# Prompt delta rule: the doubling levels on half of the columns

## The chip, the cores and the metric

The kernel runs on one core of a Trainium2 chip. The metric is device time in microseconds (us); the kernel before takes 3104.95 us, the median of 3 runs (3104.65 to 3108.51). PE is TensorE, DVE VectorE, ACT ScalarE, POOL GpSimd, SP the engine that only issues transfers.

## The reference, cut to what matters

One decoder layer is computed for 1024 prompt tokens and 64 sample tokens. The part that matters here is the gated delta rule of the prompt, for 4 heads of 128 by 128:

```python
kb = kc * bc[..., None]
m = jnp.where(strict, jnp.einsum('nbhid,nbhjd->nbhij', kb, kc) * decay, 0.0)
rhs = jnp.concatenate([vc * bc[..., None], kb * jnp.exp(gc)[..., None]], -1)
sol = lax.linalg.triangular_solve(m + jnp.eye(C), rhs, left_side=True, lower=True, unit_diagonal=True)
u, w = sol[..., :dv], sol[..., dv:]
# then, chunk after chunk: v_new = u - w S, o = (q e^g) S + qk v_new, S = S e^g_last + k' v_new
```

The kernel uses chunks of 128 tokens and does not solve the triangle row by row: it builds the inverse X of I + m by doubling the size of the blocks on the diagonal that are already inverted, from 1 to 128 in seven levels (0 to 6).

## The kernel before

The program is a row of stages with a barrier between each two. The change lies in one of them, `delta_prompt`. In it each engine has its own list of instructions in the order written, and waits on semaphores for the others.

Eight chunks are worked in four pairs `p`; the two chunks of a pair are the groups g = 0 and g = 1, with buffers of their own. Every tile is 128 partitions by 4 heads by 128 columns, so 512 columns for one instruction. For a pair the lists hold, in this order:

- Level 0: DVE multiplies `m` by the mask of level 0 into `ml` (`level_mask`, line 1725), and writes X = I - ml into `x` (L1732). PE turns X (L1496), ACT copies the result into `y` (L1611), so `y` is X transposed.
- Levels l = 1 to 6 (`level`, PE): t = ml[l]ᵀ y for g = 0 and then for g = 1 (L1547, 4 heads each, and each fp32 product is two passes, so 8 records); then for each group u = xᵀ tt (L1553) and the product for x, ttᵀ x (L1555), interleaved head by head. Between them ACT copies t from PSUM into `tt` (L1649). DVE's `update` subtracts u from `y` (L1772) and the other product from `x` (L1774); at level 6 only y is updated.
- DVE in level l: the masks of level l + 1 for both groups (L1725, 512 columns each), `update` for g = 0, `update` for g = 1, then other work that has been placed there: `gate_rows` of the next pair at l = 1 (L1686, two instructions), `decay_logs` of the next pair at l = 3 and l = 4 (L1695 to L1697, three instructions), and seven tiny instructions of a bit search for another stage (L2485 to L2487, L2390 to L2392, L2372). ACT does the counts of that search, two of 1028 columns for each level, after its two copies. PE has two wide matmuls for the next pair's gates after level 2 and two after level 3 (L1504).
- Between the pairs: the state is read, values and outputs of both chunks are made and the state is updated (L1514 to L1534 on PE, L1737 to L1761 on DVE), and the next pair's inputs are turned, scaled and multiplied (`scale_inputs`, `lower`, `first_x`). DVE's list ends this part with the mask of level 1 for g = 0, the outputs of the second chunk, and the mask of level 1 for g = 1.

PE's waits in `level` set the order around the change: t of group g at level l waits until `y` and `x` of that group are updated for level l - 1 and until its mask is made; u and the x product wait for ACT's copy.

The masks come from one line, and they say which columns can hold something:

```python
levels = [((i // (2 << l) == j // (2 << l)) & (i // (1 << l) % 2 == 1) & (j // (1 << l) % 2 == 0))
```

Row i must lie in an odd block of size 2^l and column j in an even one. So at level l half of the columns of `ml` are zero, in runs of 2^l.

Before the first pair DVE makes `gate_rows` of both chunks (L1686), copies the sums that PE made (L1780, L1782), and makes `decay_logs`, `scale_inputs`, `lower` and `first_x` of both. POOL only stores the outputs `o` of each chunk in this stage.

Of the kernel before, what the change touches and what calls it, by code (L numbers as in the profile page):

```python
# [1403 lines left out]
def over_heads(m):  # L1404

    return m.unsqueeze(1).to_broadcast([m.shape[0], GH, m.shape[1]])
# [6 lines left out]

def delta_prompt(nc, ident, ones, masks, qkv_in, beta, gate, unit, state, state_out, o_out, top, dump, squares):
# [7 lines left out]
    with ExitStack() as ctx:  # L1422
# [7 lines left out]
        ml = sc.sb("ml", [P, 2, LEVELS, GH, P])  # L1430
        sums, exps = sc.sb("sums", [P, 3, n_chunks, GH]), sc.sb("exps", [P, 3, n_chunks, GH])
# [16 lines left out]
        @block.gpsimd  # L1448
        def _(pool):
            def store(c):  # L1450
                pool.wait_ge(s["o_done"], c + 1)
                pool.dma_start(o_out[c], o[:, c % 2].rearrange("p h v -> p (h v)")).then_inc(s[f"o_stored{c % 2}"], 16)

            for c in range(n_chunks):
                store(c)
            for g in range(2):
                pool.wait_ge(s[f"o_stored{g}"], 16 * pairs)
# [144 lines left out]
        def _(act):  # L1602
# [38 lines left out]
            for p in range(pairs):  # L1641
                a, b = 2 * p, 2 * p + 1
                bit = p * bits
                for l in range(1, LEVELS):
                    for g in range(2):
                        act.wait_ge(s[f"t_done{g}"], 6 * p + l)
                        if l > 1 or p:
                            act.wait_ge(s[f"u_done{g}"], 6 * p + l - 1)
                        act.activation(tt[:, g], t_bank[g][:, :, :], ACT.Copy).then_inc(s[f"t_copied{g}"], 1)  # L1649
                    if p and l == 2:  # L1650
                        square_outputs(a - 1)
                    if p + 1 < pairs and l in (4, 5):
                        decays(2 * p + l - 2)
                    count(bit + l - 1, 0)
                    count(bit + l - 1, 1)
# [16 lines left out]
        def _(dve):  # L1672
# [46 lines left out]
            def level_mask(c, l):  # L1719
# [5 lines left out]
                dve.tensor_tensor(ml[:, g, l], m[:, g], over_heads(levels[l]), ALU.mult  # L1725
# [37 lines left out]
            def update(p, l, g):  # L1763
# [8 lines left out]
                dve.tensor_tensor(y[:, c % 4], y[:, c % 4], u_bank[g][:, :, :], ALU.subtract).then_inc(s[f"y_upd{g}"], 1)  # L1772
                if l < LEVELS - 1:
                    dve.tensor_tensor(x[:, g], x[:, g], x_bank[g][:, :, :], ALU.subtract).then_inc(s[f"x_upd{g}"], 1)  # L1774

            gate_rows(0)
            gate_rows(1)
            dve.wait_ge(s["totals"], 1)
# [1642 lines left out]
```

## Time and profile before

| | |
|---|---|
| median of 3 runs | 3104.95 us |
| the profiled execution: its own time / its span | 3107.7 us / 3105.9 us |
| busy share of PE, DVE, ACT, POOL | 91%, 50%, 29%, 7% |
| the stage `delta_prompt` in the span | 1485.4 to 1761.3 us: 275.9 us |
| PE, DVE, ACT, POOL busy in it | 226.1, 218.5, 138.5, 4.3 us |
| from the first level of the first pair to the last of the last | 1507.39 to 1737.71 us |

The profile page gives the busy time of each engine over the span and in 40 slices, and the costliest groups of instructions. The trace behind it answers for one stretch: the busy time of each engine between two times, the list of instructions in order of time with the idle time that an engine spent before each and the instruction that ended it, and the waits of one instruction for another, summed. An idle time that is not on the engine which everything else waits for costs nothing, so the stage is to be read level by level.

### The profile page before, as it was taken

What the parts mean: (1) busy time and instruction counts of PE and PEld (TensorE: products, weight loads), DVE (VectorE), ACT (ScalarE), POOL (GpSimd) and SP (SyncE); (2) the same over time, 40 slices, a digit from 0 to 9 for tenths busy, and PEclk for the clock granted to TensorE, in tenths of its full rate; (3) what the DMA queues carried; (4) which work ended last, traced back from release to release, by engine and by line L of the source; (5) the groups of instructions that cost most, each with busy time, mean ns of one, the idle gap of its engine ahead of it and who ended that gap; (6) DMA issues with size and microseconds to landing.
All of it is one profiled execution on the core that took longest, in us unless ns stands there. A gap on an engine that the chain in (4) does not pass through costs nothing. (4 is left out here: it accounts for less than half of the span.)

```text
span 3105.9 us, 44550 instructions
## 1 busy us (share of the span) xinstructions
PE 2813.8 (91%) x17345; PEld 2572.1 (83%) x17345; DVE 1552.0 (50%) x2393; ACT 889.7 (29%) x1450; POOL 221.8 (7%) x391
## 2 busy tenths in 40 slices
PE   7999999999959999868788788798879999999997
PEld 6999999999958799843687555468779999999997
DVE  5333333333444688738788678451354333333336
ACT  2111111111132557702455435341241111111111
POOL 0000000000000000015000000660000000000001
PEclk9999999999979999959899899898989999999998
DMA  3111111111031122234110101773011111111111
GB/s 108 55 41 41 45 44 48 48 42 36 6 111 35 49 74 70 85 87 103 50 43 11 53 14 32 214 224 112 14 41 55 41 54 41 43 45 46 41 41 58
DMA packets 264558, 186.55 MB, mean 60 GB/s; under 512 B 60303, under 2 KB 243807, under 8 KB 264390
## 3 DMA queue, kind: packets, MB, share of 16 engines
q1 hardware_dynamic: 212262, 112.33, 12.8%
q0 software_dynamic: 21440, 60.69, 6.0%
q10 hardware_dynamic: 30688, 11.27, 1.4%
q8 instruction: 108, 1.77, 0.2%
q14 instruction: 60, 0.49, 0.1%
HBM read 158.00 MB, written 26.22 MB: 59 GB/s over the span
## 5 line engine op out<-in xcount | busy, mean ns | idle before, releaser
L458 DVE TENSOR_TENSOR ffn_hidden<-ffn_hidden,ffn_ps_b 128x1092 f32<-128x1092 f32 x44 | 56.9, 1292 | 388.9 <-PE ffn_ps_b L85 388.9
L343 ACT ACTIVATE ffn_hi_d<-ffn_raw_d,ffn_row_mean 128x1024 fp32r<-128x1024 f32 x40 | 46.1, 1153 | 581.4 <-DVE ffn_row_mean L410 581.4
L359 ACT ACTIVATE ffn_h_hi<-ffn_hidden 128x1092 fp32r<-128x1092 f32 x44 | 49.3, 1119 | 485.3 <-DVE ffn_hidden L458 485.3
L85 PE MATMUL ffn_ps_a<-mixer_mix_hi,ffn_hi_g 128*128 128x364 f32 x528 | 117.7, 331 | 19.1 <-DVE ffn_lo_g L404 19.1
L205 POOL DMA_DIRECT2D ffn_raw_d<-in_ffn_w_down x40 | 21.3, 532 | 1593.2 <-DVE ffn_lo_d L419 1404.9
L85 PE MATMUL ffn_ps_a<-first_x_hi,ffn_hi_g 128*128 128x364 f32 x528 | 118.1, 332 | 9.5 <-DVE ffn_lo_g L404 6.1
L85 PE MATMUL proj_ps_a<-first_x_hi,proj_w_hi 128*128 128x364 f32 x336 | 79.1, 344 | 42.7 <-DVE proj_w_lo L1229 42.7
L85 PE MATMUL ffn_ps_a<-first_x_lo,ffn_hi_g 128*128 128x364 f32 x528 | 117.3, 331 | 0.0
L85 PE MATMUL ffn_ps_a<-mixer_mix_lo,ffn_hi_g 128*128 128x364 f32 x528 | 117.2, 330 | 0.0
L85 PE MATMUL ffn_ps_a<-first_x_hi,ffn_lo_g 128*128 128x364 f32 x528 | 117.0, 330 | 0.0
L85 PE MATMUL ffn_ps_b<-first_x_lo,ffn_hi_u 128*128 128x364 f32 x528 | 116.6, 329 | 0.0
L85 PE MATMUL ffn_ps_b<-first_x_hi,ffn_hi_u 128*128 128x364 f32 x528 | 116.5, 329 | 0.0
L85 PE MATMUL ffn_ps_a<-mixer_mix_hi,ffn_lo_g 128*128 128x364 f32 x528 | 116.5, 329 | 0.0
L85 PE MATMUL ffn_ps_b<-first_x_hi,ffn_lo_u 128*128 128x364 f32 x528 | 116.3, 328 | 0.0
L85 PE MATMUL ffn_ps_b<-mixer_mix_lo,ffn_hi_u 128*128 128x364 f32 x528 | 116.2, 328 | 0.0
L85 PE MATMUL ffn_ps_b<-mixer_mix_hi,ffn_hi_u 128*128 128x364 f32 x528 | 116.1, 327 | 0.0
L85 PE MATMUL ffn_ps_b<-mixer_mix_hi,ffn_lo_u 128*128 128x364 f32 x528 | 115.6, 327 | 0.0
L85 PE MATMUL ffn_ps_a<-ffn_h_hi,ffn_hi_d 128*128 128x364 f32 (+1 forms) x480 | 107.8, 333 | 5.5 <-DVE first_res L490 2.8
L85 PEld LDWEIGHTS ffn_ps_a<-mixer_mix_hi,ffn_hi_g 128*128 128x128 f32 x528 | 92.1, 190 | 20.2 <-issue 19.7
L2385 ACT ACTIVATE proj_spill<-main_scores_p,main_top_cand 128x768 bf16<-128x768 f32 (+2 forms) x96 | 99.0, 1034 | 33.5 <-DVE main_top_cand L2372 33.5
L352 ACT ACTIVATE ffn_hidden<-ffn_ps_a 128x1092 f32<-128x1092 f32 x44 | 47.6, 1083 | 212.1 <-PE ffn_ps_a L85 211.6
L85 PE MATMUL ffn_ps_b<-ffn_h_hi,ffn_hi_d 128*128 128x364 f32 (+1 forms) x480 | 106.2, 329 | 0.0
(645 smaller groups left out, 6975.4 us busy)
## 6 DMA issues: line engine op xcount, KB each, us to landing
ffn_raw_d<-in_ffn_w_down POOLq DMA_DIRECT2D x40, 512.0 KB, 3.7
proj_raw<-in_w_in SPq DMA_DIRECT2D x22, 512.0 KB, 3.8
second_ffn_raw_g<-in_ffn_w_gate SPq DMA_DIRECT2D x22, 512.0 KB, 4.1
second_ffn_raw_u<-in_ffn_w_up SPq DMA_DIRECT2D x22, 512.0 KB, 4.8
first_ffn_raw_g<-in_ffn_w_gate SPq DMA_DIRECT2D x21, 512.0 KB, 3.8
first_ffn_raw_u<-in_ffn_w_up SPq DMA_DIRECT2D x21, 512.0 KB
scratch_qkv<-proj_stage POOLq DMA_DIRECT2D x12, 544.0 KB, 3.0
delta_cur<-scratch_qkv SPq DMA_DIRECT2D x8, 768.0 KB, 5.3
```

Of the source, the lines that this page charges most:

```text
L85: last = pe.matmul(out[:, s, 0:USED[s]], w(k), x(k)[:, s * SL:s * SL + USED[s]], start=start and n == 0 and p == 0, stop=stop and n == len ...
L205: eng.dma_start(dst, src).then_inc(raw_in[kind], 16)
L343: act.activation(d_hi[:, k, :], raw["d"][:, :], ACT.Identity, bias=row_mean[:, k:k + 1]).then_inc(whi_done["d"], 1)
L352: act.activation(act_buf[:, fb, :].rearrange("p (s c) -> p s c", s=SLICES), ps_a[:, :, 0:SL], ACT.Silu).then_inc(silu_done, 1)
L359: act.activation(h_hi[:, par, fb, :], act_buf[:, fb, :], ACT.Copy).then_inc(hhi_done, 1)
L458: dve.tensor_tensor(hid, hid, ps_b[:, :, 0:SL], ALU.mult).then_inc(mul_done, 1)
L2385: act.activation(self.part(dump, i), self.score(i), ACT.Sign, bias=self.candidate(i), accum_out=self.count[:, i:i + 1]).then_inc(act_count ...
```

## The change

Masks, copies and updates of levels 1 to 6 are done on those 256 of the 512 columns that can be nonzero, through views that pick every second block of 2^l columns (`halves`). PE's matmuls keep their form and number.

- `level_mask` writes only the even blocks of `ml[l]` for l of 1 and above; level 0 is still done whole. The rest of `ml` must be zero: POOL clears all of it once, in two instructions of 3584 columns, before its first store, and DVE's first mask of each of the first two chunks waits for that.
- ACT copies only the odd blocks of t into `tt`. The rest of `tt` holds what earlier levels left there, so DVE clears `tt` once at the start, and ACT's first copy waits for that.
- `y` is updated in its odd blocks. `x` is updated in its even blocks, and since rows that are not in an odd block now get leftovers in the product, the update multiplies the product by -1 or 0 for each row: the subtraction becomes one SCALAR_TENSOR_TENSOR with a scalar for each partition, from the new tile `odd_rows`. DVE makes that tile at the start with five reductions over the masks and one small multiplication, which waits for the last of them, and the next instruction waits for the multiplication.

```diff
@@ -1411,6 +1411,16 @@
+def halves(v, l, odd):
+
+    return v.rearrange("p h (n a c) -> p (h n) a c", a=2, c=1 << l)[:, :, odd, :]
+
+
+def half_of_head(v, l, odd):
+
+    return v.rearrange("p (n a c) -> p n a c", a=2, c=1 << l)[:, :, odd, :]
@@ -1428,6 +1438,7 @@
         ml = sc.sb("ml", [P, 2, LEVELS, GH, P])
+        odd_rows = sc.sb("odd_rows", [P, LEVELS])
@@ -1451,6 +1462,8 @@
+            for g in range(2):
+                pool.memset(ml[:, g], 0.0).then_inc(s["masks_cleared"], 1)
             for c in range(n_chunks):
                 store(c)
@@ -1642,11 +1655,14 @@
                 for l in range(1, LEVELS):
+                    if l == 1 and p == 0:
+                        act.wait_ge(s["tt_cleared"], 1)
                     for g in range(2):
                         act.wait_ge(s[f"t_done{g}"], 6 * p + l)
                         if l > 1 or p:
                             act.wait_ge(s[f"u_done{g}"], 6 * p + l - 1)
-                        act.activation(tt[:, g], t_bank[g][:, :, :], ACT.Copy).then_inc(s[f"t_copied{g}"], 1)
+                        act.activation(halves(tt[:, g], l, 1), halves(t_bank[g], l, 1), ACT.Copy
+                                       ).then_inc(s[f"t_copied{g}"], 1)
@@ -1722,7 +1738,16 @@
-                dve.tensor_tensor(ml[:, g, l], m[:, g], over_heads(levels[l]), ALU.mult
+                if c < 2 and l == 0:
+                    dve.wait_ge(s["masks_cleared"], 2)
+                if l == 0:
+                    dve.tensor_tensor(ml[:, g, l], m[:, g], over_heads(levels[l]), ALU.mult
+                                      ).then_inc(s[f"level_made{g}"], 1)
+                    return
+                shape = [P, GH, P // 2 >> l, 1 << l]
+                mask = half_of_head(levels[l], l, 0).unsqueeze(1).to_broadcast(shape)
+                dve.tensor_tensor(halves(ml[:, g, l], l, 0).rearrange("p (h n) c -> p h n c", h=GH),
+                                  halves(m[:, g], l, 0).rearrange("p (h n) c -> p h n c", h=GH), mask, ALU.mult
                                   ).then_inc(s[f"level_made{g}"], 1)
@@ -1769,12 +1794,19 @@
-                dve.tensor_tensor(y[:, c % 4], y[:, c % 4], u_bank[g][:, :, :], ALU.subtract).then_inc(s[f"y_upd{g}"], 1)
+                yh, xh = halves(y[:, c % 4], l, 1), halves(x[:, g], l, 0)
+                dve.tensor_tensor(yh, yh, halves(u_bank[g], l, 1), ALU.subtract).then_inc(s[f"y_upd{g}"], 1)
                 if l < LEVELS - 1:
-                    dve.tensor_tensor(x[:, g], x[:, g], x_bank[g][:, :, :], ALU.subtract).then_inc(s[f"x_upd{g}"], 1)
+                    dve.scalar_tensor_tensor(xh, halves(x_bank[g], l, 0), odd_rows[:, l:l + 1], xh, ALU.mult, ALU.add
+                                             ).then_inc(s[f"x_upd{g}"], 1)
 
             gate_rows(0)
             gate_rows(1)
+            dve.memset(tt[:, :, :, :], 0.0).then_inc(s["tt_cleared"], 1)
+            for l in range(1, LEVELS - 1):
+                ins = dve.tensor_reduce(odd_rows[:, l:l + 1], levels[l], AX.X, ALU.max)
+            own(ins)
+            own(dve.tensor_scalar(odd_rows[:, 1:LEVELS - 1], odd_rows[:, 1:LEVELS - 1], -1.0, None, ALU.mult))
             dve.wait_ge(s["totals"], 1)
```

## Rows read from the trace of the kernel before

**Rows 1.** Busy time per stretch: levels 2, 3, 4, 5, 6 of pair 1.
```profile
1578.92:1586.05 7.13, 6.47 (x53) 5.83 (x52) 6.58 (x16) 4.63 (x14) 0.00 (x0) 1.00 0.00 1
1586.05:1592.32 6.27, 6.27 (x51) 5.80 (x50) 4.98 (x14) 3.46 (x6) 0.00 (x0) 1.00 0.01 1
1592.32:1598.98 6.66, 5.58 (x49) 5.41 (x48) 6.37 (x17) 4.63 (x7) 0.00 (x0) 1.00 0.01 2
1598.98:1605.97 6.99, 5.84 (x49) 5.51 (x49) 6.70 (x17) 4.63 (x7) 0.00 (x0) 1.00 0.00 0
1605.97:1609.97 4.00, 3.93 (x32) 3.77 (x33) 2.82 (x10) 2.24 (x5) 0.00 (x0) 1.00 0.00 0
```

**Rows 2.** Waits, 1507 to 1740 us: waiter, awaited, total us, times, longest us.
```profile
PE delta_bank_t L1547 <- DVE delta_x L1774: 11.8, 14, 1.1
PE delta_bank_t L1547 <- DVE delta_ml L1725: 5.5, 5, 1.4
```

**Rows 3.** Order of time, pair 3, end of level 3: start us, duration us, what.
```profile
1720.93 0.69 DVE L1772 TENSOR_TENSOR delta_y<-delta_y,delta_bank_u 128x512 f32<-128x512 f32 x1 [0.50 <-PE delta_bank_x L1555]
1721.54 0.68 DVE L1774 TENSOR_TENSOR delta_x<-delta_x,delta_bank_x 128x512 f32<-128x512 f32 x1
...
1722.36 1.13 PE L1547 MATMUL delta_bank_t<-delta_y,delta_ml 128*128 128x128 f32 x8 [0.66 <-DVE delta_x L1774]
```

**Rows 4.** The same view, pair 0, end of level 5.
```profile
1539.02 1.29 DVE L1725 TENSOR_TENSOR delta_ml<-delta_m,gdn_tab 128x512 f32<-128x512 f32 x2
...
1540.83 0.68 DVE L1774 TENSOR_TENSOR delta_x<-delta_x,delta_bank_x 128x512 f32<-128x512 f32 x1
...
1541.65 2.33 PE L1547 MATMUL delta_bank_t<-delta_y,delta_ml 128*128 128x128 f32 x16 [1.08 <-DVE delta_x L1774]
```

**Rows 5.** Groups of instructions, 512 columns: count, busy us, mean ns of one.
```profile
L1725 DVE TENSOR_TENSOR delta_ml<-delta_m,gdn_tab 128x512 f32<-128x512 f32 x56 | 36.6, 686 | 0.8
L1772 DVE TENSOR_TENSOR delta_y<-delta_y,delta_bank_u 128x512 f32<-128x512 f32 x48 | 32.9, 685 | 25.1 <-PE delta_bank_x L1555 20.2 <-PE delta_bank_u L1553 4.9
L1774 DVE TENSOR_TENSOR delta_x<-delta_x,delta_bank_x 128x512 f32<-128x512 f32 x40 | 27.2, 680 | 0.0
L1649 ACT ACTIVATE delta_tt<-delta_bank_t 128x512 f32<-128x512 f32 x48 | 28.6, 596 | 57.3 <-PE delta_bank_t L1547 57.3
```

**Rows 6.** The same view: 256 columns, from the sample tokens' delta rule.
```profile
L2028 DVE TENSOR_TENSOR sdelta_ml<-sdelta_m,sample_tab_s 64x256 f32<-64x256 f32 x3 | 1.1, 409 | 0.0
L2039 DVE TENSOR_TENSOR sdelta_y<-sdelta_y,sdelta_wide 64x256 f32<-64x256 f32 x2 | 0.8, 412 | 3.1 <-PE sdelta_b L1943 3.1
L1971 ACT ACTIVATE sdelta_kq_t<-sdelta_wide 128x256 f32<-128x256 f32 x1 | 0.4, 385 | 0.3 <-PE sdelta_wide L1905 0.3
```

**Rows 7.** The same view: with a scalar for each partition, two widths.
```profile
L1304 DVE SCALAR_TENSOR_TENSOR main_scores_p<-proj_spill,main_wi_tok,main_scores_p 128x512 f32<-128x512 f32 x21 | 15.1, 747 | 4.9 <-issue 2.8 <-ACT proj_spill L1130 1.9
...
L1304 DVE SCALAR_TENSOR_TENSOR main_scores_p<-proj_spill,main_wi_tok,main_scores_p 128x320 f32<-128x320 f32 x14 | 7.1, 547 | 4.1 <-ACT proj_spill L1130 2.7 <-issue 1.4
```

**Rows 8.** A copy in runs of 3 columns (min/median/max ns), and one without.
```profile
L1238 DVE COPY proj_xin<-proj_states x12: 171/176/181, 985.7 to 1181.6; 128x24 f32<-128x24 f32 x12
...
L1780 DVE COPY delta_sums<-delta_bank_t 128x64 f32<-128x64 f32 x1 | 0.2, 218 | 0.0
```

**Rows 9.** Order of time, start of the stage.
```profile
1488.45 0.69 DVE L1695 TENSOR_TENSOR delta_x<-delta_read,delta_sums 128x512 f32<-128x512 f32 x1 [1.28 <-PE delta_read L1504]
...
1499.83 0.69 DVE L1715 TENSOR_TENSOR delta_m<-delta_bank_t,delta_decay 128x512 f32<-128x512 f32 x1 [2.74 <-PE delta_bank_u L1488]
...
1501.77 0.68 DVE L1725 TENSOR_TENSOR delta_ml<-delta_m,gdn_tab 128x512 f32<-128x512 f32 x1
```

**Rows 10.** Groups of instructions elsewhere: a clear, a reduction, POOL's arithmetic.
```profile
L2246 DVE MEMSET ixs_qd<- 128x512 f32 x1 | 0.5, 485 | 4.5 <-PEq L3349 4.5
...
L2708 DVE TENSOR_REDUCE att_peak<-att_dots 128x1 f32<-128x128 f32 x8 | 2.3, 283 | 0.9 <-PE att_dots L2582 0.9
...
L800 POOL TENSOR_TENSOR ln_rows<-ln_rows,second_b_row 128x1024 f32<-128x1024 f32 x4 | 13.1, 3263 | 106.4 <-DVE ln_rows L819 106.4
```

## The prediction

> **What bounds the kernel now.** The page comes first: PE is busy for 91% of the span and DVE for 50%, so a change that leaves PE's matmuls alone can only win where PE stands and waits for somebody. The change lies in one stage of 275.9 us, so the next view is the busy time per stretch, cut at the first t product of each level [rows 1]. Read each row as length, then PE, then DVE. Three kinds of level are to be seen. Level 3 is 6.27 us with PE busy for all of it (it carries two extra gate matmuls): nothing to win. Level 2 has 0.66 us in which PE is not busy. Levels 4 and 5 have 1.08 and 1.15 us, and there DVE is busy for 6.37 of 6.66 and 6.70 of 6.99 us: DVE sets the pace, because `decay_logs` lies in its list. Who is waited for is in the summed waits [rows 2]: PE's t product waits 14 times for the update of x, 11.8 us in all, and five times for a mask, 5.5 us. The list in order of time shows the two forms of the first. In pair 3, after PE ends a level, DVE updates y and then x of group 1, and PE, having done t of group 0 meanwhile, stands 0.66 us until that is done [rows 3]. In pair 0, with decay logs in the list, the masks begin late, group 0's updates follow without a gap, and PE stands 1.08 us before t of group 0 [rows 4]. Eight waits of 0.66 and six of 1.08 make 5.3 + 6.5 = 11.8 us, which is the row's sum: four of the 0.66 precede level 2 (one for each pair), four lie in pair 3, which has no gate or decay work, and the 1.08 are the ends of levels 4 and 5 in pairs 0 to 2.
>
> **What half of the columns costs.** A mask goes from 686 ns to 409, the y update from 685 to 412 [rows 5, 6]; the rows of 256 columns are the same two operations in the sample tokens' stage, the second with PSUM as a source. The x update changes its form. With a scalar for each partition 512 columns take 747 ns and 320 take 547 [rows 7], 1.04 ns a column, so 256 take 547 - 64 x 1.04 = 480 ns against 680 now. ACT's copy goes from 596 to 385 ns. Savings: mask 0.28, y 0.27, x 0.20, copy 0.21 us. Those 256 columns come in runs of 2^l with as much left out between, down to 2 columns at level 1, and no row has runs of 2. The nearest has runs of 3: 24 columns in 176 ns, where 64 columns without gaps take 218 [rows 8]; 40 columns fewer at 1.04 give 176. So a run costs nothing that shows, and I take the prices above. The bound on the other side is that a short run costs as much as the columns it leaves out: then the half instruction takes as long as the whole one. Runs read from PSUM no row shows; they have the same two ends.
>
> **The sum, part by part.**
> (a) The eight waits of 0.66 us: the y and x updates of group 1 are the whole chain from the end of PE's products to t of group 1, so each shrinks by 0.27 + 0.20 = 0.47 and 0.19 stays. 8 x 0.47 = 3.8 us.
> (b) Levels 4 and 5 of pairs 0 to 2: DVE's list there loses two masks, two y and two x updates, 0.55 + 0.55 + 0.40 = 1.50 us, and its cycle falls from 6.98 to 5.48. PE without its wait needs 6.66 - 1.08 = 5.58, so PE is what is late next: level 4 takes 5.58, level 5 takes 5.58 and the remaining 0.19 of (a). That is 11.35 for 13.65, less 0.1 for a wait of that kind that level 6 may get: 2.2 for a pair, 6.6 us.
> (c) The first level of pairs 1 to 3: PE waits for the level-1 masks, five times. Each of these waits is one mask shorter, 5 x 0.28 = 1.4 us.
> (d) The part between the pairs: DVE settles a search bit before it goes on, and that waits for ACT's counts, which follow ACT's copies of level 6. Between 0 and 0.21 us for each of four pairs; I take 0.15, so 0.6 us. ACT's copies of the other levels are covered by t of the other group and bring nothing.
> (e) Added at the start, on DVE: a clear of 1024 columns, 2 x 0.485, five reductions of at most 0.283 [rows 10], and a tiny multiplication of at most 0.18 (the copy of 24 columns, rows 8), some 2.5 us. DVE stood idle 1.28 us just behind [rows 9], so `decay_logs` begins up to 1.3 us later. What of that reaches the first mask lies between 0 and 1.3, since DVE stands once more, 2.74 us, waiting for PE's products, which in turn wait for DVE's scaled inputs. I take 0.4. ACT's wait for the clear is over long before its first copy.
> (f) Added on POOL: two clears of 3584 columns. Their price no row shows. Its ends are 0 and POOL's arithmetic, 3.19 ns a column [rows 10], so 0 and 22.9 us for both; DVE's clear runs at 0.95 ns a column, 6.8 us for both, and being a clear it is the nearest. From the stage's opening at 1485.4 to the first mask at 1501.77 there are 16.4 us [rows 9], so I take no cost. Without that cover it is 22.9 - 16.4 = 6.5 us. Queued behind DVE's wait for it are all later masks, thus everything; behind the clears on POOL only the first store, at the end of pair 0.
> Together 3.8 + 6.6 + 1.4 + 0.6 - 0.4 = 12.0 us. The profiled execution took 3107.7 us with a span of 3105.9: it becomes 3095.7. The median lies 2.75 under that execution, so I give **3093.0**. No more can come than all waits of rows 2 and (d), 11.8 + 5.5 + 0.8 = 18.1 us, so not below 3087.
>
> **Rivals.**
> *POOL's clears are in DVE's way.* DVE's little multiplication comes at about 1489 us (where the idle time of rows 9 begins, 1487.2, with the 2.4 us of clear and reductions ahead of it, and the two small sums behind it instead of in front), while POOL is still clearing at the rate of (f). If it had to stand until the clears are over, at 1485.5 + 6.8 = 1492.3, everything behind would be up to 3.5 us later: 3096.5; with clears at POOL's arithmetic rate the first masks are 6.5 us late: 3099.5. For it: DVE's list at the start has hardly any slack. Against it: nothing in this stage shows the two engines at work at once, so the trace decides nothing. The Trainium skill has a rule for this case ("SBUF — State Buffer", section "Who interferes with whom"): a DVE instruction that uses two ports for one source, such as a multiplication by a constant from SBUF to SBUF, shares a pair of ports with GpSimd, and whoever issues first blocks the other for the whole instruction. By that rule the multiplication is such an instruction and the wait comes, while the clear of `tt` and the reductions pass. Chance 0.16.
> *Short runs are dear at levels 1 and 2 only.* Then five of the eight waits in (a) keep their length and so do the masks of (c): 2.4 + 1.4 less, 3096.8. Chance 0.09.
> *Slower: each run has a price.* The updates and masks on PE's path in (a) to (c) have some 2400 runs (1264, 360 and 768: for a y and x pair 256 at level 1, 128 at level 2 and so on down to 16 at level 5). From 12.0 / 2400 = 5 ns a run the gain is gone, from 7.6 the kernel is slower by over 0.2%; at 10 ns it would be 3105 - 12 + 24 = 3117. Against it: eight runs in rows 8 cost less than 1 ns each; for it, only that these runs are shorter and partly in PSUM. Chance 0.05.
> *The waits go but the time stays*, the change not doing what it says: PE would have to lose elsewhere what it gains, for instance by more of the first level at half of its clock, or ACT's counts would have to end last. In levels 2 to 6 of pair 1 the clock was whole, and ACT is busy 4.63 us at most in a level, under the 5.58 that PE needs. 3104 to 3106, chance 0.06.
>
> **How the numbers follow.** Forecast 3093, between 3088 and 3096.5 from (a) to (e), chance 0.64. The range 3087 to 3099 takes in the two first rivals and leaves out the last two. Two tenths of a percent, 6.2 us, is about what a measurement of this kernel can tell from no change, so faster means below 3098.7: the forecast, most of the first rival and the second, 0.64 + 0.12 + 0.08 = 0.84, rounded down to 0.82 for what I have not seen; within 0.2% 0.13; slower 0.05.
>
> **What would show it.** Masks and y updates of about 0.41 us and x updates of about 0.48, the same at level 1 as at level 5 (else the runs have a price); PE's waits for x near 0.2 us each and none of 1.08; levels 4 and 5 near 5.6 and 5.8 us; the first mask within 1 us of where it was, counted from the stage's opening, and DVE standing nowhere before its little multiplication; all other stages as before. It is wrong if DVE is seen standing beside POOL's clears, if level 1 alone stays long, or if PE's waits shrink and the stage doesn't.

## The result, and the profile after

The changed kernel takes 3087.24 us (median of seven runs, 3081.78 to 3091.53), the kernel before beside it 3103.30 us (seven runs, 3097.10 to 3108.51): ratio 0.9946, 95% interval 0.9935 to 0.9957. In a second comparison, with the experiments, it is 3089.55 against 3104.29 us, ratio 0.9959, interval 0.9945 to 0.9973. So it is faster by 13 to 16 us where 12.0 were forecast; 3087.24 us lies 5.8 us under the forecast of 3093.0 and below the 3088 that its terms allowed. The profiled execution of after took 3084.75 us with a span of 3083.1 us.

Single runs of one kernel lie some 4 us apart in stages that the change does not touch: in the first profile of after the stage opens at 1481.6 us, in the first of before at 1485.5, and in a second profile of before, taken later, at 1481.5. So stages are compared below, not spans. From the stage's opening to the read of the state in pair 3 it takes 252.2 and 253.1 us in the two profiles of before, 239.1 and 238.0 in the two of after: 14.1 us less in the mean.

The busy time per stretch of the first profile of after (stretch, length, then busy us of PE, PEld, DVE, ACT and POOL with the number of instructions, granted clock, share of the DMA engines, GB/s): the start, then levels 1 to 6 of pair 1, and the part between pairs 1 and 2, which I call the state part.

```profile
1481.50:1507.71 26.21, 17.48 (x88) 14.46 (x89) 21.36 (x39) 5.17 (x8) 6.10 (x2) 0.76 0.48 121
...
1568.30:1574.40 6.10, 5.73 (x49) 5.54 (x50) 4.17 (x14) 4.96 (x10) 0.54 (x1) 1.00 0.13 46
1574.40:1581.06 6.66, 6.45 (x52) 5.82 (x51) 5.27 (x17) 4.28 (x14) 0.00 (x0) 1.00 0.01 2
1581.06:1587.28 6.22, 6.22 (x52) 5.74 (x50) 3.52 (x14) 3.03 (x6) 0.00 (x0) 1.00 0.00 0
1587.28:1592.63 5.35, 5.35 (x49) 5.35 (x48) 4.74 (x15) 3.52 (x6) 0.00 (x0) 1.00 0.01 3
1592.63:1598.68 6.05, 5.76 (x50) 5.44 (x49) 5.31 (x16) 4.03 (x8) 0.00 (x0) 1.00 0.00 0
1598.68:1602.45 3.77, 3.77 (x32) 3.72 (x33) 2.36 (x10) 2.72 (x7) 0.00 (x0) 1.00 0.00 0
1602.45:1627.34 24.89, 19.00 (x162) 17.86 (x160) 20.74 (x45) 9.52 (x23) 0.54 (x1) 1.00 0.27 75
```

Against [rows 1], levels 2 to 6 of pair 1 are 7.13, 6.27, 6.66, 6.99 and 4.00 us before and 6.66, 6.22, 5.35, 6.05 and 3.77 after. In level 4 PE is now busy for the whole length (5.35 of 5.35) while DVE is busy for 4.74: the bound has gone from DVE back to PE, as step (b) said. The summed waits of PE show the same (waiter, awaited, total us, times, longest us), beside [rows 2]:

```profile
PE delta_bank_t L1560 <- DVE delta_ml L1749: 4.2, 5, 1.1
...
PE delta_bank_t L1560 <- DVE delta_x L1800: 2.3, 11, 0.2
```

The waits for x have gone from 11.8 us in 14 waits, the longest 1.1, to 2.3 us in 11, the longest 0.2. The five mask waits went from 5.5 to 4.2 us. The groups of instructions give the new prices, beside [rows 5] (count, busy us, mean ns of one):

```profile
L1798 DVE TENSOR_TENSOR delta_y<-delta_y,delta_bank_u 128x256 f32<-128x256 f32 x48 | 20.2, 420 | 38.8 <-PE delta_bank_x L1568 32.8 <-PE delta_bank_u L1566 5.8 <-issue 0.2
L1800 DVE SCALAR_TENSOR_TENSOR delta_x<-delta_bank_x,delta_odd_rows,delta_x 128x256 f32<-128x256 f32 x40 | 19.1, 478 | 0.0
L1664 ACT ACTIVATE delta_tt<-delta_bank_t 128x256 f32<-128x256 f32 x48 | 18.5, 386 | 49.2 <-PE delta_bank_t L1560 49.1
L1749 DVE TENSOR_TENSOR delta_ml<-delta_m,gdn_tab 128x256 f32<-128x256 f32 x48 | 18.4, 421 | 0.8
```

420, 478, 386 and 421 ns, where 412, 480, 385 and 409 were taken from other stages. All 48 masks lie between 416 and 426 ns, with runs of 2 columns as with runs of 64, and all y updates, which read PSUM, between 410 and 424: for DVE a run has no price that shows. ACT's copies take 383 to 385 ns at levels 2 to 6 and 378 to 414 at level 1, so there a run of 2 columns costs 0.03 us a copy at most.

Two rows of the first table are not in the forecast: the start is 26.21 us long where it was 21.99, and level 1 is 6.10 us at a granted clock of 1.00 where it was 7.94 at 0.79. The same view of the kernel before, its start and level 1 of its pairs 1 to 3:

```profile
1485.40:1507.39 21.99, 14.74 (x89) 11.29 (x89) 16.94 (x30) 5.17 (x8) 0.00 (x0) 0.81 0.56 144
1570.98:1578.92 7.94, 7.30 (x49) 7.11 (x49) 5.44 (x14) 4.98 (x10) 0.55 (x1) 0.79 0.09 35
1635.29:1643.29 8.00, 7.36 (x49) 7.17 (x49) 5.44 (x14) 4.98 (x10) 0.54 (x1) 0.79 0.09 34
1699.67:1708.09 8.42, 8.42 (x48) 8.40 (x49) 5.44 (x14) 5.09 (x10) 0.54 (x1) 0.64 0.09 33
```

The order of time at the start of after (start us, duration us, what, and in brackets the idle time before it and who ended it) shows why the start is longer:

```profile
1481.57 6.10 POOL L1466 MEMSET delta_ml<- 128x3584 f32 x2 [30.51 <-POOLq L3387]
1483.07 0.91 DVE L1805 MEMSET delta_tt<- 128x1024 f32 x1 [0.16 <-issue]
1483.89 0.99 DVE L1807 TENSOR_REDUCE delta_odd_rows<-gdn_tab 128x1 f32<-128x128 f32 x5
1484.92 2.78 DVE L1809 TENSOR_SCALAR delta_odd_rows<-delta_odd_rows 128x5 f32<-128x5 f32 x1
1488.10 0.68 DVE L1711 TENSOR_TENSOR delta_x<-delta_read,delta_sums 128x512 f32<-128x512 f32 x1
...
1500.16 0.69 DVE L1731 TENSOR_TENSOR delta_m<-delta_bank_t,delta_decay 128x512 f32<-128x512 f32 x1 [4.24 <-PE delta_bank_u L1501]
```

A multiplication of five columns takes 2.78 us and ends at 1487.70, in the moment in which POOL's clears do (1481.57 + 6.10 = 1487.67). Behind it the first decay log begins 6.5 us after the opening (3.0 before, [rows 9]). The clear and the five reductions run beside POOL in 0.91 and 0.99 us.

### The profile page after: what moved, and what is told of

Its sections match the earlier page's. It is cut to its first block and busy times, and to the rows that moved or that the text cites. A ratio compares the mean times of both kernels' runs of the same rounds, so it can differ in the third digit from the quotient of the medians.

```text
span 3083.1 us, 44548 instructions
## 1 busy us (share of the span) xinstructions
PE 2798.6 (91%) x17330; PEld 2561.9 (83%) x17345; DVE 1523.5 (49%) x2400; ACT 879.1 (29%) x1450; POOL 227.1 (7%) x393
## 5 line engine op out<-in xcount | busy, mean ns | idle before, releaser
L85 PEld LDWEIGHTS ffn_ps_a<-mixer_mix_hi,ffn_hi_g 128*128 128x128 f32 x528 | 92.1, 190 | 20.1 <-issue 19.6
```

The lines of the kernel that those rows point to most:

```text
L85: last = pe.matmul(out[:, s, 0:USED[s]], w(k), x(k)[:, s * SL:s * SL + USED[s]], start=start and n == 0 and p == 0, stop=stop and n == len ...
```

## The experiments

Theory A: the little multiplication has to stand until POOL's clears are over. Theory K: level 1 became shorter because PE waits less just ahead of it and so keeps its clock. The rivals are named in the expectations. e1 to e4, e6 and e10 are the changed kernel with one thing altered, e7 and e8 the changed kernel with several; e5 and e9 start from the kernel before, and two runs repeat after and before as they are.

### e1: the little multiplication in another form

```diff
-own(dve.tensor_scalar(odd_rows[:, 1:LEVELS - 1], odd_rows[:, 1:LEVELS - 1], -1.0, None, ALU.mult))
+own(dve.scalar_tensor_tensor(odd_rows[:, 1:LEVELS - 1], odd_rows[:, 1:LEVELS - 1], -2.0,
+                             odd_rows[:, 1:LEVELS - 1], ALU.mult, ALU.add))
```

> Edit: the little multiplication at the stage's start (L1809, five columns by -1, 2.78 us in the changed kernel) is written as a scalar_tensor_tensor of the same five columns (odd * -2 + odd), all else as in the changed kernel, POOL's clears with it. Theory A (a multiplication by a constant from SBUF to SBUF has to wait until POOL's clear is over, other forms don't): the new instruction takes 0.16 to 0.25 us and ends before 4 us from the stage's opening, while POOL clears until 6.1 us; the stage's start (opening to the first t product of level 1) falls from 26.2 us to between 23 and 24. Rival B (any DVE instruction at this place waits for POOL): still some 2.8 us and a start of 26.2. Rival C (the 2.78 us is the wait for the reductions' own semaphore or the price of the form, nothing of POOL): some 2.8 us, or a wait of that length ahead of it.

One run, 3088.79 us beside 3101.97 of before. The order of time:

```profile
1483.30 6.11 POOL L1466 MEMSET delta_ml<- 128x3584 f32 x2 [30.54 <-POOLq L3388]
...
1486.65 0.17 DVE L1809 SCALAR_TENSOR_TENSOR delta_odd_rows<-delta_odd_rows 128x5 f32<-128x5 f32 x1
```

0.17 us, ended 2.6 us ahead of the clears. The start is 22.5 us. Rival B falls, since another DVE instruction at this place does not wait, and of rival C the part that put the 2.78 us down to the reductions' semaphore. That the form is dear by itself, the rest of C, this run cannot exclude, because it changes the form; e2 and e6 can.

### e2: the set-up later

```diff
 gate_rows(0); gate_rows(1)
-<clear of tt, five reductions, little multiplication>
 ...
 search_start(0)
+<clear of tt, five reductions, little multiplication>
 for c in (0, 1):
     lower(c)
```

> Edit: clear of tt, five reductions and the little multiplication on DVE moved from the stage's opening to just ahead of lower(0), where DVE of the changed kernel stands 4.24 us for PE and POOL is long done. Theory A: multiplication 0.16 to 0.25 us; first decay log again 3.0 us behind the opening (6.5 in the changed kernel, 3.0 before), DVE's wait ahead of the first m shrinks to below 1 us, and the start falls from 26.2 to 22.0 (as before the change) or up to 0.4 above; the copy of the sums, an fp32 copy with PSUM as its source, runs beside POOL's clears in 0.22 us. Rival B (POOL's clears slow whatever DVE does): the copy or the decay logs take longer while POOL clears, start 24 to 26. Rival C (the multiplication is dear by itself): 2.8 us at the new place too, start near 22.5 to 24.

One run, 3091.21 us. The order of time:

```profile
1484.30 0.22 DVE L1807 COPY delta_sums<-delta_bank_t 128x64 f32<-128x64 f32 x1
...
1498.05 0.17 DVE L1821 TENSOR_SCALAR delta_odd_rows<-delta_odd_rows 128x5 f32<-128x5 f32 x1
1498.65 0.69 DVE L1731 TENSOR_TENSOR delta_m<-delta_bank_t,delta_decay 128x512 f32<-128x512 f32 x1 [0.43 <-PE delta_bank_u L1501]
```

The same instruction in its old form takes 0.17 us once POOL is done, so its form alone is not dear, and theory A is left. The copy out of PSUM runs beside the clears in 0.22, and all of the set-up fits into DVE's wait, of which 0.43 us are left. The start is 23.2 us, not the 22.0 to 22.4 that were expected: PE's transposes of the inputs took 1.06 us for four there. They take 0.60 in the first profile of before, whose start is 22.0, and 1.06 in most of the second, whose start is 22.8, so the start without the change scatters in the same way. In e7, with the same set-up, it is 22.0.

### e3: POOL's clears in fourteen pieces

```diff
 for g in range(2):
-    pool.memset(ml[:, g], 0.0).then_inc(s["masks_cleared"], 1)
+    for l in range(LEVELS):
+        pool.memset(ml[:, g, l], 0.0).then_inc(s["masks_cleared"], 1)
 ...
-dve.wait_ge(s["masks_cleared"], 2)
+dve.wait_ge(s["masks_cleared"], 2 * LEVELS)
```

> Edit: POOL's two clears of 3584 columns are cut into fourteen of 512, the same area. Theory A1 (the little multiplication waits for the one POOL instruction that is running): it takes at most 0.16 plus one short clear, 0.3 to 0.8 us, and the start falls by some 2 to 2.5 us to about 24. Theory A2 (POOL keeps the way as long as it has one clear behind the other): the multiplication ends when the last clear does, 2.8 us or a little more if fourteen clears take longer than two. If fourteen clears cost POOL much more than 6.1 us (over 0.15 us more for each), the first mask is still not reached before 20 us.

One run, 3085.40 us. The order of time:

```profile
1481.40 6.58 POOL L1467 MEMSET delta_ml<- 128x512 f32 x14 [30.53 <-POOLq L3388]
...
1484.75 3.25 DVE L1810 TENSOR_SCALAR delta_odd_rows<-delta_odd_rows 128x5 f32<-128x5 f32 x1
```

The multiplication stands through some seven of POOL's instructions, which follow each other every 0.47 us, and ends when the last one does (1488.00 and 1487.98). So A2 holds: cutting POOL's work into short instructions didn't let DVE in while one followed the other without a gap.

### e5 and e6: the two halves of the change alone

e5 keeps the half masks and POOL's clears, and takes back the copies, the updates and DVE's set-up; e6 keeps these and takes back the masks and the clears:

```diff
 e5:
-act.activation(halves(tt[:, g], l, 1), halves(t_bank[g], l, 1), ACT.Copy)
+act.activation(tt[:, g], t_bank[g][:, :, :], ACT.Copy)
-<half updates of y and x>
+<whole updates of y and x>
 e6:
-for g in range(2):
-    pool.memset(ml[:, g], 0.0).then_inc(s["masks_cleared"], 1)
-if l == 0:
+if l >= 0:          # every mask whole
```

> Edit: of the change only the half masks (and POOL's clears they need) remain; copies and updates are whole as before, without the clear of tt, the reductions and the little multiplication. By the prediction's own terms: DVE's list in levels 4 and 5 loses two masks, 0.55 us for each level, 3.3 us in pairs 0 to 2; the level-1 mask waits lose 1.4 us; the eight waits of 0.66 stay. Sum 4.7 us, so 0.9985 of the kernel before; stage start as before, 22.0 to 22.7 us, since nothing of the two-port form stands beside the clears. Theory K2 (the clock at level 1 of pairs 1 to 3 falls by chance, less often with the shorter mask waits: so far in 8 of 12 levels with half masks it stayed at 1.00, in 1 of 6 with whole ones): two of three level 1 at about 7.0 or below, some 2 us more, 0.998. Rival (masks gain nothing until the updates are short as well): levels 4 and 5 stay at 6.66 and 6.99, 0.9995 or more.

> Edit: of the change only the half copies and updates remain (with the clear of tt, the reductions and the little multiplication on DVE); masks are whole and POOL clears nothing. By the prediction's own terms: eight waits of 0.66 become 0.19 (3.8 us); DVE's list in levels 4 and 5 loses two y and two x updates, 0.94 us, so these levels are 5.7 and 6.05 long (1.9 us a pair, 5.7 us); state part 0.3; start 0.4 to 1.3 dearer. Sum 8.5 to 9.4 us, 0.997. Theory A for the start: without POOL's clears the little multiplication takes 0.17 us at its old place (2.78 in the changed kernel) and the start is 22.5 to 23.3 us instead of 26.2. Rival: it still takes 2.8. The clock at level 1 of pairs 1 to 3: with the long mask waits (1.42 and 0.65) it should mostly fall, 7.4 to 8 us a level, as before the change; if it stays at 1.00 in two of three, the length of the wait says nothing.

e5: 3097.01 us against 3104.29, ratio 0.9975, interval 0.9965 to 0.9985. e6: 3093.80 us, ratio 0.9960, interval 0.9945 to 0.9975. The busy time of levels 4 and 5 of pair 1 in e5:

```profile
1589.33:1595.47 6.14, 5.58 (x50) 5.42 (x48) 5.85 (x17) 4.36 (x6) 0.00 (x0) 1.00 0.01 3
1595.47:1601.92 6.45, 5.83 (x48) 5.51 (x49) 6.16 (x17) 4.64 (x8) 0.00 (x0) 1.00 0.00 0
```

The same two levels in e6:

```profile
1587.42:1593.14 5.72, 5.52 (x49) 5.36 (x48) 5.35 (x16) 3.88 (x6) 0.00 (x0) 1.00 0.01 3
1593.14:1599.36 6.22, 5.60 (x49) 5.44 (x49) 5.93 (x17) 4.21 (x8) 0.00 (x0) 1.00 0.00 0
```

Two masks fewer take 0.52 and 0.54 us from these levels (0.55 expected), two y and x updates fewer 0.94 and 0.77 (0.94). Each half pays by itself, as it should where DVE's list is the bound. Together with level 6 they save 1.05 and 2.06 us a pair, and both at once 2.48: the last 0.6 us are lost because PE is late by then. Level 1 of pairs 1 to 3 in e5 takes 6.84, 6.12 and 8.37 us, so theory K2's two of three came. The starts are 22.7 and 22.6 us. The little multiplication of e6, at its old place and with no clears on POOL:

```profile
1487.10 0.17 DVE L1805 TENSOR_SCALAR delta_odd_rows<-delta_odd_rows 128x5 f32<-128x5 f32 x1
```

In e6 POOL's clears and the half masks are gone, and with them the 2.8 us; in e5 the clears are there and no instruction of that form. Both agree with A, and e6 speaks once more against rival C.

### Level 1 and its clock: e4, the repeats, e9 and e10

e4 makes only the level-1 masks whole again:

```diff
-if l == 0:
+if l <= 1:
```

> Edit: only the level-1 masks are whole again (512 columns), four halves of the change stay. It puts the 0.28 us for each mask back into the wait ahead of the first t product of pairs 1 to 3. Theory K (the unforeseen gain at level 1 is the clock: PE stands 1.14 and 0.37 us in the changed kernel, 1.42 and 0.65 before, and with the shorter wait the granted clock of this level stays 1.00 where it was 0.79): level 1 of pairs 1 and 2 goes back from 6.10 us at 1.00 to 7.6 to 7.9 at about 0.8, so 1.3 to 1.8 us for each pair with two masks at 0.28 in it. Rival (the clock differs from run to run whatever the wait): level 1 at 6.1 to 6.7 us with a clock of 1.00, so at most 0.56 us a pair.

One run, 3086.82 us. Level 1 of pairs 1, 2 and 3:

```profile
1568.69:1576.12 7.43, 7.16 (x49) 6.86 (x50) 4.44 (x14) 4.61 (x10) 0.54 (x1) 0.77 0.10 37
1629.35:1635.72 6.37, 5.73 (x48) 5.54 (x49) 4.45 (x14) 4.57 (x10) 0.54 (x1) 1.00 0.11 42
1688.96:1696.01 7.05, 7.05 (x49) 7.03 (x50) 4.45 (x14) 4.68 (x10) 0.54 (x1) 0.77 0.11 40
```

One kernel, the same instructions, and the level is 6.37 us at 1.00 or 7.05 to 7.43 us at 0.77: PE's 5.73 us of work become 7.1 when a part of it runs at 1.2 instead of 2.4 GHz. Theory K in its strict form (a longer wait always lets the clock fall) does not hold for pair 2. So the next runs asked whether it is chance alone. A second profile of each kernel:

> The changed kernel as it is, beside the others: 0.9946 of the kernel before (0.9935 to 0.9957 earlier). In its profile: start 24 to 26.5 us with the little multiplication at 2.8 us again; level 1 of pairs 1 to 3 either near 6.1 us at a clock of 1.00 or near 7.1 to 7.4 at 0.77. Theory K2 (chance): not the same pairs as in the first profile (there pairs 1 and 2 at 1.00, pair 3 at 0.76). Rival (fixed by place): again pair 3 alone.

> The kernel before as it is, for a second profile. In question is level 1 of pairs 1 to 3, whose clock was 0.79, 0.79 and 0.64 in the first profile (7.94, 8.00 and 8.42 us). Theory K2 (whether the clock falls there is chance, whatever the mask waits of 1.42 and 0.65 us): at least one of the three at 1.00 and then about 6.6 us long, as in the two kernels with whole masks so far (2 of 6). Rival K (the longer waits always let it fall): all three at 0.8 or less and 7.4 us or more. Start 22.0 us, waits of 0.66 and 1.08 us ahead of the t products as in the first profile in any case.

After again: 3089.55 us (above), start 24.7 us with the multiplication at 2.78, level 1 at 0.77, 1.00 and 0.77: pair 3 again, and now pair 1 too. Before again: 3104.95 us in one run, level 1 of pairs 1 to 3 at 7.91, 7.99 and 8.38 us and 0.78, 0.79 and 0.64, all three low as in the first profile, so the chance theory K2 missed here. Counted over all profiles with half masks and a first wait of 1.14 us (two of after, e1, e2, e3, e5), 10 of 18 levels stay at 1.00; with whole masks and 1.4 us (two of before, e4, e6) 2 of 12. But the two groups differ in more than the wait: it is 9 of 15 with both halves of the change and 1 of 3 in e5, 2 of 6 in e4 and e6 and none of 6 in before. The last two runs therefore take the wait away and lengthen it, and leave the columns of every mask, copy and update as they were. e9 is the kernel before with the order of work of e8 (below), which takes the wait away; e10 is the changed kernel with

```diff
+pad = sc.sb("pad", [P, GH, P])
 ...
+for i in range(2):
+    own(dve.tensor_tensor(pad[:, :, :], m[:, 0], over_heads(levels[1]), ALU.mult))
 level_mask(a + 2, 1)
```

> Edit: the kernel before (whole masks, copies and updates) with the order of work of e8 at the end of a pair: level-1 and level-2 masks of the next pair early, search bits 6 and 7 in gaps. Nothing is halved. In question is the clock of level 1 in pairs 1 to 3: 1.00 in none of six levels of the kernel before, where PE stands 1.42 and 0.65 us ahead of the two t products, in three of three of e8, where it does not. Theory K3 (PE's wait just ahead of level 1 is what lets the clock fall): 1.00 in at least two of the three levels, and these take 6.0 to 6.5 us (7.9 to 8.4 before). Rival (the whole copies and updates, thus PE's waits inside the level, let it fall): 0.8 or less in two or three, 7.4 us or more. The start without POOL's clears and DVE's set-up: 21.9 to 22.9 us.

> Edit: the changed kernel with two more multiplications of 512 columns on DVE, into a tile of its own that nobody reads, ahead of the first level-1 mask of pairs 1 to 3. They leave all results as they are and lengthen PE's wait ahead of level 1 from 1.14 to about 2.5 us. Theory K3 (PE's wait just ahead of level 1 is what lets the clock fall): the granted clock of level 1 is below 0.85 in all three pairs, and it takes 7.0 us or more from the first t product. Rival (chance, or the length of the other work): 1.00 in one or two of three, as in the changed kernel (10 of 18 levels in the kernels with half masks so far), 5.8 to 6.3 us there. State part 24.9 + 1.4 = 26.2 to 26.3 us.

Level 1 of pairs 1 to 3 in e9 (one run, 3091.56 us beside 3107.93 of before):

```profile
1568.63:1574.38 5.75, 5.68 (x49) 5.52 (x49) 5.36 (x14) 3.22 (x6) 0.54 (x1) 1.00 0.13 48
1629.13:1634.89 5.76, 5.69 (x50) 5.52 (x49) 5.36 (x14) 3.23 (x6) 0.54 (x1) 1.00 0.12 47
1689.65:1695.40 5.75, 5.68 (x49) 5.52 (x49) 5.35 (x14) 3.22 (x6) 0.54 (x1) 1.00 0.13 48
```

In e10 (one run, 3095.42 us) the order of time shows PE's wait ahead of level 1 of pair 1:

```profile
1569.98 1.36 PE L1561 MATMUL delta_bank_t<-delta_y,delta_ml 128*128 128x128 f32 x8 [2.59 <-DVE delta_ml L1750]
```

The busy time of level 1 of its pairs 1 to 3:

```profile
1569.98:1577.35 7.37, 7.20 (x49) 6.91 (x49) 4.18 (x14) 3.49 (x8) 0.54 (x1) 0.77 0.10 38
1631.77:1638.97 7.20, 7.20 (x48) 7.04 (x49) 4.17 (x14) 3.49 (x8) 0.54 (x1) 0.76 0.10 36
1693.38:1700.50 7.12, 7.12 (x48) 7.12 (x49) 4.18 (x14) 3.50 (x8) 0.54 (x1) 0.76 0.10 39
```

No wait ahead: 1.00 in six of six levels (e8, described next, and e9). 1.14 us: 10 of 18. 1.4 us: 2 of 12. 2.59 us: none of three. In e7, also described next, PE stands 2.15 us inside the level instead, and one of three stays at 1.00. So the clock fell more often the longer PE stood just ahead of level 1. That is a tendency over few levels: at the rate of 8 falls in 18, three of three would come by chance about once in eleven times, an estimate from these counts. It is no rule either, since at 1.14, at 1.4 and in e7 one kernel shows both. In e9 copies, updates and masks are all whole, so their length alone does not let it fall; but e8 and e9 also take ACT's counts and the level-2 masks out of level 1, and e10 is the one run in which little but the wait was made longer. What decides where one kernel shows both stays open.

### e7 and e8: what a better order is worth

e7 adds to e2 an order in which PE's mask waits go away (cut to the end of a pair; level 1 of the next pair then makes no level-2 masks any more):

```diff
     first_x(b + 2)
+    level_mask(a + 2, 1)
+    level_mask(b + 2, 1)
 search_end(bit + 6)
 search_start(bit + 7)
-level_mask(a + 2, 1)
 outputs(b)
-level_mask(b + 2, 1)
+level_mask(a + 2, 2)
+level_mask(b + 2, 2)
 search_end(bit + 7)
```

> Edit on the changed kernel: DVE's set-up moved to just ahead of lower(0), and at the end of a pair both level-1 masks of the next pair are made ahead of the search bit, both level-2 masks ahead of the next search bit. Expected: start 22 to 23.2 us instead of 26.2 (3 to 4 us); level 1 of pairs 1 to 3 begins without the waits of 1.14 and 0.37 us: its first t product 1.0 to 1.1 us earlier counted from the pair's read of the state, and the updates of level 1, which DVE reaches after two search bits, at most 0.5 to 1 us earlier in the end, so 0.5 to 1.1 us a pair, 1.5 to 3.3 us. Together 4.5 to 7 us under the changed kernel, ratio to the kernel before 0.9930 where the changed kernel has 0.9946. Rival 1: the search bits come later by the masks' 0.84 us and become the bound, so that level 1 grows by what its start gains: only the start's 3 to 4 us remain, 0.9935. Rival 2 (start and pairs are decided by the clock): less than 2 us.

3090.37 us against 3104.29, ratio 0.9958, interval 0.9946 to 0.9971: no better than the changed kernel beside it (0.9959). The start is 22.0 us and the wait of 1.14 us is gone, but level 1 of pairs 1 to 3 takes 7.89, 9.52 and 9.51 us (6.1 to 7.4 in after). The order of time in pair 2:

```profile
1626.31 2.07 PE L1560 MATMUL delta_bank_t<-delta_y,delta_ml 128*128 128x128 f32 x16
...
1627.81 1.15 ACT L2511 ACTIVATE cut_bias_s<-index_scores_s,index_top_s_cand 128x1028 bf16<-128x1028 f32 x1 [0.70 <-DVE index_top_s_cand L2405]
...
1630.10 0.65 ACT L1664 ACTIVATE delta_tt<-delta_bank_t 128x256 f32<-128x256 f32 x2
...
1630.53 0.49 PE L1566 MATMUL delta_bank_u<-delta_tt,delta_x 128*128 128x128 f32 x2 [2.15 <-ACT delta_tt L1664]
```

Both t products are done by 1628.4, but ACT's two counts for a search bit stand in its queue ahead of the copies. They begin when DVE has settled the bit before, which the two early masks in front of it (0.75 us) delay, and PE stands 2.15 us. This is rival 1, and worse than it: the wait was moved and made longer, and behind it the clock fell in two of the three pairs (0.82; 1.00 in pair 1). e8 moves the counts as well:

```diff
 e8, ACT:
+count(bit + 6, 0); count(bit + 6, 1)
 new_values(a)
 copy_qk(a + 2); copy_qk(b + 2)
-count(bit + 6, 0); count(bit + 6, 1)
+count(bit + 7, 0); count(bit + 7, 1)
 ...
 first_y(a + 2); first_y(b + 2)
-count(bit + 7, 0); count(bit + 7, 1)
 e8, DVE:
 outputs(a)
+search_end(bit + 6); search_start(bit + 7)
 residuals(b)
 ...
-search_end(bit + 6); search_start(bit + 7)     # where e7 has it
```

> Edit on e7 (set-up later, level-1 and level-2 masks early): ACT makes the counts of search bit 6 ahead of the new values of chunk a (it stands 4.4 us there) and those of bit 7 where bit 6 was, so that none lies between the first y and the copies of level 1; DVE settles bit 6 behind the outputs of chunk a, where it stands 2.1 us for the read of the state, and bit 7 at the end of the pair. Theory (e7 lost its gain because ACT's two counts, 2.3 us, stand in front of the copies that PE waits for): level 1 of pairs 1 to 3 takes 5.7 to 5.8 us where the clock is 1.00 and 6.9 to 7.2 where it is half for a part (e7: 7.9 and 9.5), the state part stays at 23.6 us (24.9 in the changed kernel), start 22 to 23.2. Against the changed kernel 1.6 us for each of three pairs and 2 to 4 us at the start, 7 to 9 us: ratio 0.992 to 0.993. Rival 1 (DVE's or ACT's work is only moved on): the state part grows by the 1.3 us of the search bit, and 2 to 4 us of the start remain, 0.995. Rival 2 (PE, with less idle time, is held at half its clock for longer): level 1 at 8 us or more.

3081.67 us (3079.92 to 3086.91) against 3104.41, ratio 0.9928, interval 0.9914 to 0.9941. The state part and level 1 of pair 2:

```profile
1600.02:1623.68 23.66, 18.84 (x163) 17.94 (x161) 20.82 (x45) 10.96 (x25) 0.54 (x1) 1.00 0.28 79
1623.68:1629.16 5.48, 5.48 (x51) 5.43 (x49) 3.93 (x14) 3.54 (x6) 0.54 (x1) 1.00 0.13 49
```

PE is busy for all of level 1, at full clock in all three pairs, and the state part is 1.2 us shorter than in after. From the opening to the read of the state in pair 3 it takes 228.8 us, 9.8 less than after. This is the fastest version here. e9 shows what the order is worth without the change: 241.0 us for that stretch where the kernel before needs 252.6, so 11.6 us, beside the 14.1 that the change gives without the order.

## Why the prediction was wrong, and where it was right

Two steps failed. Step (e) gave the start 0.4 us, and it cost 2.9 in the mean, mainly because DVE's little multiplication stood until POOL's clears were over. And step (c) counted only waits at level 1 and took PE's own busy time there as fixed, without a reason: 0.6 us were forecast for this stretch and 4.2 measured, nearly all of the rest being PE's time at a higher granted clock. Steps (a), (b) and (d) hold in their mechanism. By stretches, each the mean of two profiles of before and two of after:

| stretch | steps | forecast | before | after | measured |
|---|---|---|---|---|---|
| levels 2 to 6, all pairs | (a), (b) | -10.4 | 122.8 | 111.4 | -11.4 |
| state parts, three | (c) in part, (d) | -1.3 | 76.0 | 74.7 | -1.3 |
| level 1 of pairs 1 to 3 | (c), second masks | -0.6 | 24.3 | 20.1 | -4.2 |
| start and level 1 of pair 0 | (e), (f) | +0.4 | 29.5 | 32.4 | +2.9 |

**(a) right.** The waits of 0.66 us are 0.21 now. **(b) right, 0.3 us a pair too small.** Levels 4 to 6 of pair 1 went from 17.65 to 15.17 us, 2.48 where 2.2 were forecast. Levels 4 and 5 together came as the step says, 11.40 us for 11.35, but in other parts: level 4 takes 5.35 and not 5.58, level 5 takes 6.05 and not 5.77. The 0.3 us are level 6, which got 0.23 shorter where 0.1 was taken off for a new wait. e5 and e6 show each half of DVE's saving by itself. **(c) and (d) right** in the waits they name (1.3 for 1.4 us, and 0.42 us a state part for 0.28 + 0.15). The two parts of the latter come apart in e6, where the masks are whole: a state part takes 25.32 us before, 25.18 in e6 and 24.90 after.

**(e) was mis-sized, and with it the first rival.** 0.4 us was the forecast for the start. The stretch up to the first t product, 22.0 and 22.8 us in the two profiles of before, is 26.2 and 24.7 in those of after, and 22.5 in e1, where nothing stands. The 1.5 us between the two profiles of after are no part of the stand: DVE's last wait of the start is 4.24 us in the first and 2.74 in the second, and PE's transposes ahead of it took 1.12 and 1.06 us for four in the first, 0.66 and 0.60 in the second. The clear, the reductions and the copy of the sums did what the step says; the little multiplication, taken at 0.18 us at most, stood 2.6 us beside POOL's clears. The rival had the mechanism, its place and nearly its price (up to 3.5 us; the first decay log is 3.5 us later), and a chance of 0.16. The Trainium skill's page "SBUF — State Buffer", section "Who interferes with whom", says that a DVE multiplication by a constant between tiles in SBUF may take a pair of ports that it shares with GpSimd, and is then blocked for the whole of a GpSimd instruction that began before, while an instruction with two inputs there is blocked only by one that reads. The runs agree on which forms wait (2.78 us against 0.17 in e1, and 0.17 without the clears in e6). On how long they differ: the wait lasts over instruction after instruction of POOL (e3, 3.25 us with pieces of 0.47). The step should have counted the rule as likely: that the trace decides nothing was no reason for a low chance, since nothing in it spoke against the wait.

(f) was right: the clears take 6.1 us, where 6.8 were taken from DVE's clear, and end long before the first mask.

**What no step had: the clock in level 1.** The forecast counted the level-1 masks as 0.28 us each and took PE's work in this level as given. The 4.2 us measured are mostly PE's own time: 5.7 us of products at 1.00, 7.1 to 8.4 at 0.64 to 0.79. The fourth rival named the first level's clock, but only as something to lose, and read it in levels 2 to 6, where it was whole. The row of level 1 of pair 1 before, 7.30 us busy at 0.79, stands nowhere in the working; 7.30 x 0.79 = 5.8 would have bounded the gain at 1.5 us for such a level. Which of the edits brings the clock back is not shown (above). It is no sure gain: in the six profiles with half masks and a wait of 1.14 us one or two of the three levels keep their clock.

**The bound of 18.1 us**, "not below 3087", was wrong in kind: it added up PE's waits and took its busy time as fixed, and level 1 gave 4.2 us where its waits gave 0.6. That the median stayed just above it says nothing for it. Of the rivals, the two on the price of runs fell with the prices above. (The third counts the runs of six level-1 masks where (c) has five waits; with five it is 2264 runs and 5.3 ns a run, which changes nothing.)

**The sum.** -12.0 us forecast (with the fourth part of (d), which lies behind these stretches), -14.1 measured in the stage. Levels 2 to 6 missed by -1.0 us, level 1 by -3.6 and the start by +2.5, and the last two hid one another for the most part; that the stage came within 2.1 us of the sum is luck. The rest of the way from 3093.0 to 3087.24 is that the kernel before was 3103.30 and not 3104.95 beside it, and the scatter of the runs.

## What to carry to other kernels

Where the work in one engine's list sets the pace, count the instructions in it: each one that gets shorter saves its full difference until another engine is late. Before a small instruction is put beside another engine's long one, look whether the two share something: a multiplication of five columns stood 2.6 us here, and 0 when it was moved behind the clears or put in another form. A wait that is taken away ahead of TensorE's work is worth its length and, where the granted clock had fallen behind it, the time at the lower clock as well; but look at what stands next in every queue (here ACT's counts) before moving the work that ended it.

## What the runs showed of the hardware that was not expected

- A DVE multiplication by a constant, five columns, stood until POOL's clears were over, also where these were fourteen in a row without a gap (3.25 us, through the last seven or so). A clear, five reductions, a form with two inputs from SBUF and a copy from PSUM ran beside such clears in 0.91, 0.99, 0.17 and 0.22 us.
- POOL clears 3584 columns in 3.08 us, 0.86 ns a column, a little less than DVE's 0.89 (912 ns for 1024); its arithmetic takes 3.19 [rows 10]. Fourteen clears of 512 columns cost 6.58 us, two of 3584 cost 6.10.
- Level 1 of one kernel takes 6.1 or 7.1 to 7.4 us with the same instructions, by the clock; how often it fell went with PE's wait just ahead (0 us: 0 of 6; 1.14: 8 of 18; 1.4: 10 of 12; 2.59: 3 of 3; and 2 of 3 in e7, where the wait of 2.15 us lies inside the level). That the wait alone decides it is not shown.
- Access in runs of two columns with two left out cost DVE nothing that shows, from PSUM either, and ACT 0.03 us a copy at most: the masks take 416 to 426 ns and the y updates 410 to 424 at all levels, ACT's copies 378 to 414 at level 1 and 383 to 385 at the others.
